# Last down-projection with five instead of four weight tiles in seven block products, and half of the low parts of 19 weight tiles made by GpSimd

## The reference, cut to what matters

```
up = centred_dwconv(h2 @ w_up[l], conv_w_ffn[l], conv_b_ffn[l])     # w_up: 1024 x 5632
a, v = jnp.split(up, 2, axis=-1)
ffn_out = (jax.nn.gelu(a) * v) @ w_down[l]                          # w_down: 2816 x 1024
h_res = h_res + rmsnorm_2(ffn_out, g_ffn_post[l])
```

## Time and profile before

| what | value |
|---|---|
| median of 3 runs | 937.82 us (935.09 to 939.82) |
| the profiled execution, its time | 935.25 us |
| its span, first to last instruction | 933.6 us |
| PE busy | 925.4 us, 99% |
| DVE busy | 749.6 us, 80% |
| ACT busy | 608.5 us, 65% |
| POOL busy | 36.8 us, 4% (15 instructions) |
| granted TensorE clock | 0.998 |

### The profile page before, as it was taken

The page is one execution under the profiler, slowest core; times in us unless marked ns, Lnnn a source line. Parts: engine busy times, 40 slices in busy tenths (PEclk is TensorE's granted clock), DMA queues, the critical chain, the costliest instruction groups (busy, mean ns, idle before and its releaser), DMA issues.

```text
span 933.6 us, 14799 instructions
## 1 busy us (share of the span) xinstructions
PE 925.4 (99%) x5994; PEld 825.1 (88%) x5994; DVE 749.6 (80%) x1100; ACT 608.5 (65%) x895; POOL 36.8 (4%) x15
## 2 busy tenths in 40 slices
PE   9999999999999999999999999999999999999997
PEld 7888888888888888888888888999999999999886
DVE  4998846888999867746887999876468789899997
ACT  7675648888565668748888555734555596666553
POOL 0011250000000000020000000000000000000000
PEclk9999999999999999999999999999999999999999
DMA  8554254554466453445555556454544436555451
GB/s 309 224 182 174 93 181 180 180 184 178 182 224 225 181 180 118 153 169 184 192 181 180 180 207 235 157 200 162 181 157 162 178 136 238 191 181 181 173 188 45
DMA packets 25635, 168.23 MB, mean 180 GB/s; under 512 B 2848, under 2 KB 3936, under 8 KB 5984
## 3 DMA queue, kind: packets, MB, share of 16 engines
q1 hardware_dynamic: 25136, 166.84, 49.4%
q10 hardware_dynamic: 432, 0.46, 0.2%
HBM read 166.24 MB, written 1.05 MB: 179 GB/s over the span
## 4 chain that ended last, share of the span: by engine, by line
PE 98%; DVE 0%; DMA 0%; ACT 0%; issue 0%; DVEq 0%; SPq 0%; ACTq 0%
PE bank L753 24%; PE bank L754 23%; PE bank L755 23%; PE bank L876 13%; PE bank L880 7%; PE bank L781 1%; DMA h<-x_rows 0%; PE bank L930 0%; PE bank L934 0%; PE bank L938 0%; PE bank L1305 0%; PE bank L1197 0%; PE bank L1179 0%; PE bank L1171 0%; PE bank L1048 0%; PE bank L1015 0%
## 5 line engine op out<-in xcount | busy, mean ns | idle before, releaser
L2133 DVE TENSOR_TENSOR wlo<-raw,whi 128x2048 fp32r<-128x2048 f32 (+2 forms) x126 | 280.5, 2228 | 94.8 <-ACT whi L1462 94.5
L1462 ACT ACTIVATE whi<-raw 128x2048 fp32r<-128x2048 f32 (+1 forms) x133 | 252.8, 1904 | 75.8 <-PE bank L755 74.0
L876 PE MATMUL bank<-nhl,whi 128*128 128x512 f32 x512 | 124.0, 392 | 0.0
L876 PEld LDWEIGHTS bank<-nhl,whi 128*128 128x128 f32 x512 | 94.0, 188 | 18.7 <-issue 0.7
L754 PE MATMUL bank<-mlo,whi 128*128 128x258 f32 x368 | 103.9, 282 | 0.0
L753 PE MATMUL bank<-mhi,whi 128*128 128x258 f32 x368 | 103.9, 282 | 0.0
L755 PE MATMUL bank<-mhi,wlo 128*128 128x258 f32 x368 | 103.8, 282 | 0.0
L753 PE MATMUL bank<-nhl,whi 128*128 128x258 f32 (+3 forms) x320 | 92.3, 288 | 0.0
L754 PE MATMUL bank<-nhl,whi 128*128 128x258 f32 (+3 forms) x320 | 91.5, 286 | 0.0
L755 PE MATMUL bank<-nhl,wlo 128*128 128x258 f32 (+3 forms) x320 | 90.6, 283 | 0.0
L1475 ACT ACTIVATE th<-tr 128x1024 fp32r<-128x1024 f32 x40 | 42.5, 1062 | 51.6 <-PE bank L755 34.0
(11 more groups left out here) (422 smaller groups left out, 1983.6 us busy)
## 6 DMA issues: line engine op xcount, KB each, us to landing
raw<-w_stream SPq DMA_DIRECT2D x153, 1024.0 KB, 4.8
raw<-w_stream SPq DMA_DIRECT2D x3, 512.0 KB, 7.8
h<-x_rows SPq DMA_DIRECT2D x4, 256.0 KB, 5.0
cst<-consts SPq DMA_DIRECT2D x1, 832.0 KB, 6.3
raw<-w_stream SPq DMA_DIRECT2D x2, 256.0 KB, 5.2
e<-g_post SPq DMA_DIRECT2D x1, 512.0 KB, 5.6
out_rows<-e SPq DMA_DIRECT2D x2, 256.0 KB, 2.0
raw<-w_stream SPq DMA_DIRECT2D x1, 352.0 KB, 9.0
```

Of the source, the lines that this page charges most:

```text
L876: return pe.matmul(us[c].t[:, :], w[:, k, c * P:c * P + P].hi, nboth[:, k, :], start=k == 0, stop=k == 7)
L1462: act.activation(whi[j][:, 0:n], raw[j][:, 0:n], ACT.Copy).then_inc(s_hi.up(i))
L2133: dve.tensor_tensor(wlo[j][:, 0:m], raw[j][:, 0:m], whi[j][:, 0:m].bitcast(F32), ALU.subtract).then_inc(s_lod.up(i))
```

## The change

Tile `DOWN2 + 2` (147) joins the tiles done in seven block products, so five of the eleven are. Its weight combinations have no place in the loop over `it`, which starts too late for them, and are written out by hand: `combined(2, 2)` at the head of DVE's iteration 20, `combined_hi(2, 2)` after `gelu(21)`, `combined_lo(2, 2)` after `ff_mul(21)`; `hi` and `lo` of tile 147 move from iteration 21 to the end of the epilogue of the loop, behind `ff_hi(21)` and `ff_lo(21)`. A fifth buffer of block sums is laid over constants that are no longer used. Where the next tile is treated too (147 and 152), PE now takes `block_combinations` first. For tiles `UP2 + 5` to `DOWN2 + 1` (128 to 146), `cut` gives DVE 1024 columns and POOL the other 1024.

```diff
-SEVENS = (..., (3, 5, 7, 8))
+SEVENS = (..., (2, 3, 5, 7, 8))
@@ cut(i)
+    if UP2 + 5 <= i < DOWN2 + 2:
+        return n // 2
     return n if i < OUT_AB + 2 or C0 - 1 <= i < OUT_C + 4 or i >= IN2 else n // 2
@@ buffers
+        o_spare = o_cst + 4 * CST["gmask"][0]
+        ASP[2].append(Pair(at("bsh4", 512, o_spare, F32R), at("bsl4", 512, o_spare + 2048, F32R)).view(FOUR, a=2, b=2))
@@ seven_products (PE)
-                if l < 2 and it + 1 in SEVENS[l]:
+                if it + 1 in SEVENS[l]:
                     block_combinations()
                     weight_blocks()
@@ down_hi (ACT)
-                if it + 1 in SEVENS[l]:
+                if it + 1 in SEVENS[l] and (l, it) != (2, 1):
                     combined_hi(l, it + 1)
@@ ACT, loop over n
-                if n >= 3:
+                if 3 <= n < 21:
                     hi(UP2 + n + 3)
...
             gelu(21)
+            combined_hi(2, 2)
             ff_hi(20)
             ff_hi(21)
+            hi(DOWN2 + 2)
@@ DVE, loop over n
-                if n >= 2:
+                if n == 20:
+                    combined(2, 2)
+                if 2 <= n < 21:
                     lo(UP2 + n + 3)
...
             ff_mul(21)
+            combined_lo(2, 2)
             ff_lo(20)
             ff_lo(21)
+            lo(DOWN2 + 2)
```

More of the change, by code:

```diff
@@ L244 @@
 SECOND_DFT = {4: 0, 8: 1, 12: 2, 14: 3}
-SEVENS = ((2, 4, 5, 7, 8, 10, 12, 13), (2, 4, 5, 7, 8, 10, 12, 13), (3, 5, 7, 8))
+SEVENS = ((2, 4, 5, 7, 8, 10, 12, 13), (2, 4, 5, 7, 8, 10, 12, 13), (2, 3, 5, 7, 8))
 DOWNS = (*DOWN, DOWN2)
```

## The result

| | before | after |
|---|---|---|
| median | 935.66 us (6 runs, 935.09 to 939.82) | 942.86 us (6 runs, 942.15 to 945.48) |
| the profiled execution, its time | 935.25 us | 942.47 us |
| its span | 933.6 us | 940.7 us |

The ratio is 1.0073, 95% interval 1.0054 to 1.0091: slower, by 7.2 us on the profiled executions. The three runs of before that the forecast had to go by had a median of 937.82 us; with three more it is 935.66 us. So the forecast of 942.0 us came near (942.86 measured) partly by luck: it stood on a base that was 2.2 us too high, and its loss of 4.2 us was too small by 3 us.

The account below looks back on a forecast made before the run. PE was taken to bound the kernel, with DVE nearly full; POOL's uncovered time and tile 147's new DVE work outweighed PE's 0.68 us, a net loss of 4.2 us on the median of 937.82: 942.0 us, range 936.5 to 944.6.

Parts of the forecast that it names:

- PE's gain of 0.68 us: Tile 147 loses 3 matmuls of 0.227 us each on PE: the whole direct gain, 0.07% of the time.
- One engine stands for the whole of the other's instruction, both ways: In the loop, POOL's 2.2 us subtraction and DVE operations with two SBUF inputs block each other; whoever is first runs through.
- Rival A: A DVE subtraction passes while POOL runs, PE waits for nothing, gain 0.68 us: 937.1 us; chance 0.24.
- The uncovered part: POOL's 2.2 us less 0.91 of convolution steps: 1.3 up to 2.2 us on DVE per iteration, against 1.08 saved.
- How late DVE is: DVE's lag from iterations 12 to 18: 0.9 us behind at iteration 19, or 4.4 if the uncovered part averages 1.8.
- The work behind the lag: DVE's queue from `lo(145)` to the end of `lo(148)`: 23.6 us, plus 2.6 (early end) or 1.3 (late) for POOL.
- It can't run away: DVE's lag stays bounded: late, it meets POOL elsewhere, and PE needs an up tile only 11.5 us after its slot came free.
- rival C: DVE's operations keep POOL from starting; PE waits for up tiles, each from 141 adding up to 1 us: 945 to 950; chance 0.06.
- The end of `lo(148)` sets the loss: At tile 148 the loss is the end of `lo(148)` less 885.7: 2.8 us early, 5.0 late, 4.2 taken.
- The two waits at tile 148: PE waits for `lo(148)`, then for the combinations of 148: about 2 and 1.3 us.
- Costed at nothing: SP's slot reloads about 1.2 us later, ACT's later `hi(147)`, and PE's other order in tiles 147 and 152: no cost.
- The chances: For the whole kernel's time: slower 0.33, same 0.64, faster 0.03; a measurement tells no less than about 0.5%, 4.7 us.

Follow-up runs that it names:

- e4: The whole change, but POOL writes zeros into its half of the low parts instead of subtracting, reading nothing: 934.77 us, ratio 0.9994.
- e11: The change, POOL starting after DVE's half, DVE's four convolution steps first, combinations of 148 split before the low part of 149: 935.25 us, ratio 1.0007.
- e3: The whole change, but POOL's half of the low parts of tiles 128 to 146 is made by nobody: 935.18 us, ratio 0.9995.
- e2: The kernel before, plus only POOL making half of the low parts of tiles 128 to 146: 937.64 us, ratio 1.0025.
- e1: The kernel after without POOL's help: fifth tile in seven products alone, DVE making all low parts: 937.39 us, ratio 1.0021.
- e10: e6, with PE's order in tiles 147 and 152 as before the change (weight blocks first): 937.76 us, ratio 1.0012.
- e6: e1, with DVE splitting combinations before the following tile's low part, and making `lo(148)` before forming that tile's combinations: 935.56 us, ratio 1.0000.
- e7: The whole change with 512 instead of 1024 columns of each low part on POOL: 937.97 us, ratio 1.0028.
- e8: The whole change, but POOL starts its half only when DVE's half of the same tile is done: 942.87 us, ratio 1.0082.

## Why the prediction was right, and where it was short

**PE's gain of 0.68 us: right by the count, not shown by the times.** 5991 matmuls instead of 5994, each 0.227 us. Where nothing waits, the profiled spans are 933.0 us in e4 and 932.7 in e11, against 933.6, but 934.3 in e3, and no interval tells the gain from nothing.

**One engine stands for the whole of the other's instruction, both ways: right.** The step for which no row of before existed. The loop product at 788.86 shows it, e2 that it needs nothing else of the change, e4 that a fill, which reads nothing, doesn't do it. Rival A (a DVE subtraction passes) fell. The price of one POOL part was 2.4 us, not 2.2. The uncovered part, summed from the groups: the product 28.7 us over its 22 against 9.2 (19.5), `lo` 27.2 against the 23.2 of e3 (4.0), block sums' low parts 2.2, the operation of 512 columns 1.8, and the convolution steps of the first two iterations, whose inputs both lie in SBUF, 2.0. That is 29.5 us for 19 tiles, 1.55 each, within my 1.3 to 2.2, against 1.07 saved.

**How late DVE is: too small, the term that was mis-sized.** The loss was given as 2.8 to 6.3 us and is 7.2. I let DVE be on time at iteration 12 and gave it 0.9 to 4.4 us of lag by iteration 19. But POOL meets it from iteration 2 on. The `lo` of tile 138 (iteration 12) started at 821.15 before and at 825.04 after, already 3.9 us late; that of tile 141 was 7.9 us late (839.16 and 847.04), that of tile 145 5.1 us (861.38 and 866.45), with another 1.4 us of standing in it. The first iterations, which DVE before did in 4.70 us each (773.67 to 778.37) to catch up with PE, now took 5.02 (776.78 to 781.80), and each block sum came on top. The work behind the lag was sized well: from the start of `lo(145)` to the end of `lo(148)` it was given as 24.9 to 26.2 us and took 26.06 (866.45 to 892.51).

**"It can't run away": wrong for one tile.** When DVE is late ACT is too, and then makes two high parts in quick succession, so POOL's parts come close together: at 840.78 and 844.18 us. DVE stood at both, 2.90 us for a low part of block sums and 2.56 for the operation of 512 columns. PE waited 0.7 us for tile 141. That is what rival C said PE would do, but not for its reason: POOL wasn't kept from starting (ACT's high part took from 838.80 to 840.71 us, POOL began at 840.78). It was DVE's half that came late, at 847.04.

**The end of `lo(148)` sets the loss: right.** By the rule (end of `lo(148)`) - 885.7 the loss for the measured end, 892.5 us, is 6.8 us; the profiled executions differ by 7.2. The two waits at tile 148 were given as about 2 and 1.3 us and are 2.05 and 0.92. That I put the end at 888.5 to 890.7 is the lag above, and the waits for tile 147 (1.61 and 0.45 us), which I had only said lie inside it, are its other face.

**Costed at nothing: right where it was said.** SP's later reloads and ACT's later `hi` of 147 caused no wait of PE; ACT waited once for a landing, 1.24 us at 893.18, and e1, without POOL, has such a wait too. The other order on PE is worth 1.7 us by the waits of e10 against e6, 1.1 us by ratios whose intervals overlap; the forecast counted nothing for it.

**The chances.** 0.64 for "within 0.5%" and 0.33 for slower: the measured 0.73% is in the smaller share. The range to 944.6 us held the time, but only on the high base: the same loss of up to 6.3 us on 935.66 ends at 942.0, with the 0.5 of spread at 942.5, and 942.86 lies above it. The mechanism was right and the size of the lag was not.

## What to carry to other kernels

In this kernel, work moved from DVE to GpSimd was free only where it read nothing from SBUF or ran beside DVE operations with at most one SBUF input; what wasn't so covered was added to DVE's queue, and showed there as busy time of small operations, not as a wait. Count the covered stretch before moving work: 2.4 us of POOL with 0.7 us of cover lost 7 us in 19 tiles and the work behind them, the same with 1.6 us of cover lost nothing that could be measured. And before a saving on the bound engine (0.68 us here) is bought with work on an engine that is 94% busy, look at what that engine's queue holds ahead of the next thing the bound engine wants: moving two low parts in it was worth 1.5 us by PE's waits (e1 against e6), twice the saving.

## What the runs showed of the hardware that was not expected

- A busy time can hold the standing: the DVE product of 0.42 us is shown as 1.80 us busy when it meets POOL, with no idle before it. POOL's parts, which nearly always came first in the loop, show about 2.4 us. Where POOL came second, in e7, it is POOL's time that holds the standing (2.86 us).
- TensorE's clock. In e8 PE issued nothing from 875.57 to 878.54 us, and the matmuls behind it stand 0.43 us apart instead of 0.227, until about 885 us:

```profile
870.00:878.00 8.00, 5.96 (x29) 4.57 (x27) 7.83 (x15) 3.48 (x8) 1.91 (x1) 0.99 0.38 133
878.00:885.00 7.00, 6.46 (x16) 5.11 (x17) 6.79 (x14) 3.91 (x8) 0.43 (x1) 0.52 0.43 150
885.00:892.00 7.00, 6.92 (x31) 5.36 (x29) 6.93 (x10) 6.30 (x6) 0.00 (x0) 1.00 0.35 128
```

  The clock, the third number from the right, fell to the lower of its two levels (1.2 instead of 2.4 GHz). 14 matmuls at 0.2 us more are 2.8 us, as much as the wait itself. In e8 this didn't lengthen the whole, since PE had to wait for `lo(148)` anyway. In the change PE's longest pauses, 2.4 and 2.0 us from start to start, left the clock at 1.00.
